# Gate and up projections of a hybrid decoder layer: three of eight row pairs as seven block products, with a reordered group and the gate function on ScalarE

## The chip, the cores and the metric

The kernel runs on one core of one Trainium2 chip. The metric is the device time of one execution in microseconds (us). A core has TensorE (PE in the rows), which multiplies; VectorE (DVE) and ScalarE (ACT), which work element by element; GpSimd (POOL); and SyncE (SP), which here issues the weight loads. The engines run their own instruction lists in order and wait for each other through semaphores.

## What is computed

One decoder layer on 256 tokens with a model width of 2048, then a final RMSNorm. Before the part that the change touches there is a combined input projection, three kinds of token mixing and an output projection. The part that matters here is the feed-forward block, whose hidden width is 5632:

```
hf = rms_norm(x, norm_ffn)
gate, up = jnp.split(hf @ w_gu, 2, axis=-1)      # w_gu: 2048 x 11264
return x + (jax.nn.silu(gate) * up) @ w_down     # w_down: 5632 x 2048
```

`silu(g)` is `g * sigmoid(g)`, which is also `0.5 * g * (1 + tanh(g / 2))`.

## The kernel before

All products are fp32-like. Each operand is split into a high part (fp32r, a rounded fp32) and a low part (the rest), and a product of blocks is three matmuls: high by high, high by low of the weights, low by high (`ff_product`, L1691). The 128 x 128 block of activations is the stationary operand, a 128 x 512 block of weights the moving one.

The gate and up projections are 11 groups of 512 columns each of gate and of up. In a group, the 2048 rows of the weights are 8 row pairs (k = 0 to 7) of 2 x 128 rows. A **unit** is one row pair of gate or of up: 128 x 1024 numbers, 512 KB, loaded by one DMA into one of four `raw` buffers. ScalarE copies it to `w_hi` (`ff_high`, L644), VectorE writes raw minus high to `w_lo` (`ff_low`, L1176), TensorE multiplies it with the two token blocks b = 0, 1 and the two row blocks: 12 matmuls. `w_hi` and `w_lo` are rings of four slots, so ScalarE may fill a slot only when TensorE has used the slot four before it (`unit_used`), and a load may refill a `raw` buffer only when VectorE has read it (`lo_ready`).

For a row pair in **seven** form (kind "seven"), gate and up of the row pair are treated together as a 2 x 2 by 2 x 2 block product and done with 7 block products instead of 8 (Winograd's form of Strassen's scheme): 21 matmuls in place of 24. It takes four slots of the ring: the gate unit, half of the up unit, and two slots with sums of weight blocks. The sums are made by three VectorE operations (`ff_weight_sums`, L1188), and are then split in high and low as well (`ff_sum_high`, L650; `ff_sum_low`, L1182). The matching sums of the activations are made once (`ff_summands`, L1127). Seven products use the four `mx` PSUM banks and three `acc` banks; after the last "seven" of a group the common parts are added to the right sums (`fold_gate`, `fold_up`, L1211 and L1222).

Group 0 has no "seven". The groups j = 1 to 10 follow the table `FF_ORDER` (L61), each entry (kind, k, i, v): row pair k, load number i, ring slot v. Here two row pairs are "seven". All engines follow the same table, each with its own work between the entries:

- After the first unit of a group, TensorE transposes the 8 blocks of the product silu(gate) * up of the group before (`act_transposed`, L1669) into `mx`; ScalarE copies them to `actT_hi` (`act_high`, L625); VectorE makes `actT_lo` (`act_low`) and four sums for the down projection (`act_sums`, L1110).
- VectorE makes the product itself (`activate_folded`, L1077): an add and a multiply for each token block, the second pair only when TensorE has finished the group.
- The gate function: ScalarE computes tanh of half the gate (`gate_tanh`, L616), VectorE finishes it with (tanh + 1) * gate (`gated`, L1067).

The activations are kept at full precision in `hT_hi` and `hT_lo`. The groups are a hardware loop with one group per turn on ScalarE, VectorE and TensorE; SyncE's list is unrolled.

Of the kernel before, what the change touches and what calls it, by code (L numbers as in the profile page):

```python
# [14 lines left out]
F32 = mybir.dt.float32  # L15
# [49 lines left out]
FF_SLOT_OF = [-4, -3, -2, -1] + [v + d for kind, _k, _i, v in FF_ORDER for d in ((0, 1) if kind == "seven" else (0,))]  # L65
# [65 lines left out]
def hybrid_layer(nc, x, norm_mix, w_in, gla_a2, gla_ab, gla_norm, ml_conv, ml_ib, ml_fb, ml_norm,  # L131
                 sgu_ln_g, sgu_ln_b, sgu_w, sgu_b, w_out, norm_ffn, w_gu, w_down, norm_final, out):
    ctx = ExitStack()
    with ctx:
# [16 lines left out]
        half_rs_h, half_rs2_h = stat[:, 18:20], stat[:, 20:22]  # L151
# [121 lines left out]
        def _(sp):  # L273
# [75 lines left out]
        def _(pool):  # L349
# [81 lines left out]
            pool.wait_ge(sem("gate_used"), 2 * NG_FF)  # L431
            pool.wait_ge(sem("x1_stored"), 16 * NB)
# [10 lines left out]
        def _(act):  # L443
# [172 lines left out]
            def gate_tanh(used, gates_read=None):  # L616
# [8 lines left out]
            def act_high(groups, c):  # L625
                act.wait_ge(sem("actT_psum"), groups)
                act.activation(actT_hi[:, bass.ds(c, 4), :].rearrange("p c t -> p (c t)"),
                               mx[:, 0:2, :].rearrange("p k n -> p (k n)"), ACT.Copy).then_inc(sem("act_hi"), 1)

            def first_gate_up():  # L630
                for k in range(2 * UPG):
# [17 lines left out]

            def ff_sum_high(j, d, v, made):  # L650

                act.wait_ge(sem("ff_w_sums"), j * 4 + (made - 4))
                act.wait_ge(unit_used, j * FF_SLOTS + (FF_BASE + v - R + 1))
                act.activation(w_hi[:, v % R, :], ff_sum[:, d, :, :].rearrange("p k n -> p (k n)"), ACT.Copy)\  # L654
                   .then_inc(hi_ready, 1)

            def gate_up(j):
                for kind, k, i, v in FF_ORDER:
                    if kind == "up" and k == 4:
                        act.wait_ge(unit_used, j * FF_SLOTS + (FF_BASE + 12))  # L660
                        act.wait_ge(lo_ready, j * FF_SLOTS + (FF_BASE + 13))
# [6 lines left out]
                    if kind == "gate" and k == 5:  # L668
                        act_high(j, j * 4 - 4)
                    if kind == "up" and k == 6:  # L670
                        act.wait_ge(sem("gate_folded"), j * 2)
                        gate_tanh(j * FF_SLOTS + (FF_BASE + 14), j * 2)

            first_gate_up()
            with act.Fori(1, NG_FF) as j:
                gate_up(j)
# [67 lines left out]
        def _(dve):  # L744
# [332 lines left out]
            def activate_folded(groups, used):  # L1077

                for b in range(NB):
# [10 lines left out]
                    dve.scalar_tensor_tensor(out=act_tok[:, b, :], in0=up_part(b), scalar=half_rs2_h[:, b:b + 1],  # L1090
# [3 lines left out]
            def activate(used, gates_done):  # L1094
# [3 lines left out]
                for b in range(NB):  # L1098
                    dve.scalar_tensor_tensor(out=act_tok[:, b, :], in0=acc[:, 2 + b, :], scalar=half_rs2_h[:, b:b + 1],
# [3 lines left out]
            def act_low(groups, c, summed=False):  # L1103
# [4 lines left out]
                   .then_inc(sem("act_lo_made" if summed else "act_lo"), 1)  # L1108

            def act_sums(j, g):  # L1110

                a11, a12_, a21_, a22_ = (mx[:, 0, c * P:(c + 1) * P] for c in (0, 2, 1, 3))
                s1, s3 = (s_32[:, g, i, :].rearrange("p g n -> p (g n)") for i in range(2))
                c = bass.ds(j * 4 - 4, 1)
                s2, s4 = (t[:, c, P:2 * P].rearrange("p c t -> p (c t)") for t in (actT_hi32, actT_lo32))
                dve.wait_ge(sem("act_lo_made"), j)
                dve.tensor_copy(s4, a21_).then_inc(sem("a21_kept"), 1)
                dve.wait_ge(sem("a21_kept"), j)
                dve.tensor_tensor(s1, a22_, s4, ALU.add).then_inc(sem("s1_made"), 1)
# [25 lines left out]

            def ff_summands_low():
# [4 lines left out]
                                  ff_sum[:, 1, :, :].rearrange("p k n -> p (k n)"), flat, ALU.subtract)\  # L1151
                   .then_inc(sem("ff_lo_ready"), 1)

            def first_gate_up():
                for k in range(2 * UPG):
# [8 lines left out]
                    if k == 11:  # L1164
                        dve.wait_ge(sem("rs_h_ready"), 1)
                        step(dve.tensor_tensor(half_rs2_h, rs_h, rs_h, ALU.mult))
                        dve.tensor_scalar(half_rs_h, rs_h, 0.5, None, ALU.mult).then_inc(sem("rs_h2_ready"), 1)
                        settle()
                        step(dve.tensor_scalar(half_rs2_h, half_rs2_h, 0.5, None, ALU.mult))
                        settle()  # L1170
                        gated(0)
                    if k == 13:
                        ff_summands()
                ff_summands_low()

            def ff_low(j, i, v, c0=0):  # L1176

                dve.wait_ge(hi_ready, j * FF_SLOTS + (FF_BASE + v + 1))
                dve.tensor_tensor(w_lo[:, v % R, c0:UC * GW], raw[:, i % R, c0:UC * GW],  # L1179
                                  w_hi[:, v % R, c0:UC * GW].bitcast(F32), ALU.subtract).then_inc(lo_ready, 1)  # L1180

            def ff_sum_low(j, d, v):  # L1182

                dve.wait_ge(hi_ready, j * FF_SLOTS + (FF_BASE + v + 1))
                dve.tensor_tensor(w_lo[:, v % R, :], ff_sum[:, d, :, :].rearrange("p k n -> p (k n)"),
                                  w_hi[:, v % R, :].bitcast(F32), ALU.subtract).then_inc(lo_ready, 1)

            def ff_weight_sums(j, i, k, opening=False):  # L1188

                a = i % R  # L1190
                for slot in range(2):
                    dve.wait_ge(loaded[a + slot], j * (16 * 2 * UPG // R) + 16 * ((U_FF + i) // R + 1))
                if k == 1:
# [664 lines left out]
```

## Time and profile before

| | us |
|---|---|
| median of 3 runs | 1102.86 (1102.61 to 1103.05) |
| the profiled execution | 1103.19 |
| its span, first to last instruction | 1101.5 |
| PE busy in the span | 1090.1 (99%) |
| DVE busy | 864.0 (78%) |
| ACT busy | 580.9 (53%) |
| mean granted TensorE clock | 0.998 of full speed |

The profile is of one execution. Matmuls overlap: a 128 x 512 one is shown as 0.39 us long, but the next one starts long before it ends, so the time of a stretch of TensorE is read from the starts. For the same reason "busy" of PE does not tell how fast it goes. DVE and ACT operations overlap a little as well (a row "x4 4.74" is four operations in 4.74 us). In the rows, "<-" after an idle time names what the engine waited for.

### The profile page before, as it was taken

The numbers are of one execution on the slowest core, as the hardware profiler recorded it, in microseconds if no ns is written. First come the engines' busy times: TensorE is split into PE (matmuls) and PEld (weight loads), VectorE is DVE, ScalarE is ACT, GpSimd is POOL, SyncE is SP. The second block draws the span as 40 slices with busy tenths as digits, with TensorE's granted clock in tenths as the row PEclk, the third lists the DMA queues.
The fourth block names the chain that finished last, engine by engine and source line by source line (L and its number), as shares of the span: only waits on it lengthen the run. The fifth ranks groups of instructions, "written<-read, shape, count | busy, mean of one in ns | idle before, by whom it ended". The sixth has DMA issues, their size and how long they took to land.

```text
span 1101.5 us, 13909 instructions
## 1 busy us (share of the span) xinstructions
PE 1090.1 (99%) x5101; PEld 906.9 (82%) x5101; DVE 864.0 (78%) x1061; ACT 580.9 (53%) x705; POOL 40.6 (4%) x68
## 2 busy tenths in 40 slices
PE   8999999999999999999999999999999999999997
PEld 7897889888888888888888888888888888888885
DVE  5556866688756557988988888889888899899896
ACT  5655545555445444545545545546455556546553
POOL 2600000000010000000000000000000000000000
PEclk9999999999999999999999999999999999999999
DMA  8765646465546575656657557566565766666663
GB/s 285 217 197 168 189 128 183 154 172 153 190 176 223 178 267 171 211 171 215 202 158 230 167 174 241 175 192 210 170 212 194 282 203 216 199 200 213 195 226 116
DMA packets 110941, 215.31 MB, mean 195 GB/s; under 512 B 6956, under 2 KB 11632, under 8 KB 110000
## 3 DMA queue, kind: packets, MB, share of 16 engines
q1 hardware_dynamic: 108976, 205.36, 59.2%
q0 software_dynamic: 1632, 8.96, 2.2%
q8 instruction: 28, 0.46, 0.2%
q10 hardware_dynamic: 288, 0.39, 0.1%
q14 instruction: 17, 0.14, 0.0%
HBM read 210.49 MB, written 4.19 MB: 195 GB/s over the span
## 4 chain that ended last, share of the span: by engine, by line
PE 96%; DVE 2%; DMA 1%; issue 1%; SPq 0%; ACT 0%; POOLq 0%; POOL 0%; ACTq 0%; DVEq 0%
PE acc L1693 11%; PE acc L1694 11%; PE acc L1695 11%; PE acc L1413 11%; PE acc L1414 11%; PE acc L1415 11%; PE acc L1758 5%; PE acc L1759 5%; PE acc L1760 5%; PE mx L1405 2%; PE mx L1693 2%; PE mx L1694 2%; PE mx L1695 2%; PE mx L1758 1%; PE mx L1759 1%; PE mx L1760 1%
## 5 line engine op out<-in xcount | busy, mean ns | idle before, releaser
L759 DVE TENSOR_TENSOR w_lo<-raw,w_hi 128x1024 fp32r<-128x1024 f32 (+2 forms) x144 | 166.7, 1169 | 117.8 <-ACT w_hi L454 117.0
L454 ACT ACTIVATE w_hi<-raw 128x1024 fp32r<-128x1024 f32 (+2 forms) x143 | 143.4, 1013 | 135.0 <-PE acc L1415 132.7
L648 ACT ACTIVATE w_hi<-raw 128x1024 fp32r<-128x1024 f32 (+1 forms) x160 | 158.4, 1005 | 94.4 <-PE acc L1695 86.7
L1693 PE MATMUL acc<-w_hi,hT_hi 128*128 128x512 f32 x520 | 203.3, 391 | 0.0
L1179 DVE TENSOR_TENSOR w_lo<-raw,w_hi 128x1024 fp32r<-128x1024 f32 (+1 forms) x160 | 180.5, 1154 | 29.0 <-ACT w_hi L648 27.2
L1694 PE MATMUL acc<-w_lo,hT_hi 128*128 128x512 f32 x520 | 202.4, 389 | 0.0
L1695 PE MATMUL acc<-w_hi,hT_lo 128*128 128x512 f32 x520 | 202.3, 389 | 0.0
L1413 PE MATMUL acc<-w_hi,hT_hi 128*128 128x512 f32 (+2 forms) x416 | 157.7, 379 | 0.0
L1415 PE MATMUL acc<-w_hi,hT_lo 128*128 128x512 f32 (+2 forms) x416 | 155.5, 374 | 0.0
L1414 PE MATMUL acc<-w_lo,hT_hi 128*128 128x512 f32 (+2 forms) x416 | 155.5, 374 | 0.0
L1695 PEld LDWEIGHTS acc<-w_hi,hT_lo 128*128 128x128 f32 x520 | 97.6, 188 | 20.5
L1693 PEld LDWEIGHTS acc<-w_hi,hT_hi 128*128 128x128 f32 x520 | 97.6, 188 | 20.0
L1694 PEld LDWEIGHTS acc<-w_lo,hT_hi 128*128 128x128 f32 x520 | 97.7, 188 | 20.0
L692 ACT ACTIVATE w_hi<-raw 128x1024 fp32r<-128x1024 f32 x88 | 83.3, 970 | 34.4 <-PE acc L1760 18.8
L1280 DVE TENSOR_TENSOR w_lo<-raw,w_hi 128x1024 fp32r<-128x1024 f32 x88 | 94.6, 1111 | 6.1 <-ACT w_hi L692 3.9
L1760 PE MATMUL acc<-w_hi,actT_lo 128*128 128x512 f32 x250 | 97.3, 389 | 0.0
L1758 PE MATMUL acc<-w_hi,actT_hi 128*128 128x512 f32 x232 | 90.5, 390 | 0.0
L1759 PE MATMUL acc<-w_lo,actT_hi 128*128 128x512 f32 x232 | 90.3, 389 | 0.0
L1415 PEld LDWEIGHTS acc<-w_hi,hT_lo 128*128 128x128 f32 x416 | 78.2, 188 | 14.0
L1413 PEld LDWEIGHTS acc<-w_hi,hT_hi 128*128 128x128 f32 x416 | 78.2, 188 | 13.9 <-ACT tok L479 0.4
L1414 PEld LDWEIGHTS acc<-w_lo,hT_hi 128*128 128x128 f32 x416 | 78.2, 188 | 13.1
L654 ACT ACTIVATE w_hi<-ff_sum 128x1024 fp32r<-128x1024 f32 x40 | 42.5, 1063 | 73.9 <-PE acc L1695 60.8
(299 smaller groups left out, 1553.3 us busy)
## 6 DMA issues: line engine op xcount, KB each, us to landing
raw<-in_w_gu SPq DMA_DIRECT2D x176, 512.0 KB, 4.2
raw<-in_w_down SPq DMA_DIRECT2D x88, 512.0 KB, 4.5
raw<-in_w_in SPq DMA_DIRECT2D x79, 512.0 KB, 3.9
raw<-in_w_out SPq DMA_DIRECT2D x32, 512.0 KB, 4.3
raw<-in_w_in SPq DMA_DIRECT2D x8, 272.0 KB, 2.8
raw<-in_w_in SPq DMA_DIRECT2D x8, 264.0 KB, 2.8
x<-in_x POOLq DMA_DIRECT2D x2, 1024.0 KB, 8.0
x_kept<-x POOLq DMA_DIRECT2D x2, 1024.0 KB, 6.1
```

Source lines behind the costliest of these rows:

```text
L648: act.activation(w_hi[:, v % R, c0:UC * GW], raw[:, i % R, c0:UC * GW], ACT.Copy).then_inc(hi_ready, 1)
L759: dve.tensor_tensor(w_lo[:, slot, 0:UC * width], raw[:, slot, 0:UC * width], w_hi[:, slot, 0:UC * width].bitcast(F32), ALU.subtract).then_ ...
L1179: dve.tensor_tensor(w_lo[:, v % R, c0:UC * GW], raw[:, i % R, c0:UC * GW], w_hi[:, v % R, c0:UC * GW].bitcast(F32), ALU.subtract).then_inc ...
L1413: pe.matmul(o, hi[:, c + i, tb], wh, start=first and i == 0, stop=False)
L1414: pe.matmul(o, hi[:, c + i, tb], wl, start=False, stop=False)
L1415: ins = pe.matmul(o, lo[:, c + i, tb], wh, start=False, stop=last and i == UC - 1)
L1693: pe.matmul(o, a[0], w[0], start=first, stop=False)
L1694: pe.matmul(o, a[0], w[1], start=False, stop=False)
L1695: return pe.matmul(o, a[1], w[0], start=False, stop=last)
L1758: pe.matmul(o, a[0], w[0], start=first, stop=False)
L1759: pe.matmul(o, a[0], w[1], start=False, stop=False)
L1760: return pe.matmul(o, a[1], w[0], start=False, stop=last)
```

## The change

Five edits in the gate and up projections:

1. A third row pair (k = 2) becomes "seven" in each of the groups 1 to 10. Its activation sums are made once, at the end of group 0 (`third_summands`), and kept in a part of `actT_hi` and `actT_lo` that is not used until the last group. The plain units of k = 2 fall away.
2. The table: three gate units stand ahead of the first "seven" instead of four, and "seven" 2 stands after the unit up 3. A group now has 22 slots instead of 20, which is not a multiple of four, so slots are numbered by the parity of the group (`ring`), and the hardware loops take two groups per turn (4 turns for groups 2 to 9; groups 1 and 10 are written out).
3. Loads are issued in order of use. The gate and up units of "seven" 0 and 1 now lie in `raw` buffers 3 and 0, so `ff_weight_sums` reads the pair as `raw[:, 3::-3, ...]`, with a negative step between two rows of 512.
4. The gate function is one ScalarE operation per token block, `Silu`; `gated` on VectorE is gone, and the scale factors are simpler.
5. VectorE's own order in a group: `activate_folded` comes after the second unit's low part instead of the third's; the weight sums of "seven" 0 come ahead of `act_low` and `act_sums`, not behind them; the copy of block a21 goes to ScalarE; `fold_gate` stands before up 6 and `fold_up` after up 7.

```
-FF_ORDER = [("gate", 2, 0, 0), ("gate", 3, 1, 1), ("gate", 4, 2, 2), ("gate", 5, 3, 3), ("seven", 0, 4, 4),
-            ("gate", 6, 6, 8), ("gate", 7, 7, 9), ("seven", 1, 8, 10)] + [("up", k, 8 + k, 12 + k) for k in range(2, UPG)]
-FF_SLOTS = 20
+FF_SUMMED = 3
+FF_ORDER = [("gate", 3, 0, 0), ("gate", 4, 1, 1), ("gate", 5, 2, 2), ("seven", 0, 3, 3), ("gate", 6, 5, 7), ("gate", 7, 6, 8),
+            ("seven", 1, 7, 9), ("up", 3, 9, 13), ("seven", 2, 10, 14)] + [("up", k, 8 + k, 14 + k) for k in range(4, UPG)]
+FF_SLOTS = 22
...
+def ring(j, v):
+    return (v + 2 * ((j[1] - 1) % 2)) % R
...
-                    act.activation(gate_s[:, b, :], acc[:, b, :], ACT.Tanh, scale=half_rs_h[:, b:b + 1])\
-                       .then_inc(sem("gate_tanh"), 1)
+                    act.activation(gate_s[:, b, :], acc[:, b, :], ACT.Silu, scale=rs_h[:, b:b + 1])\
+                       .then_inc(sem("gate_used"), 1)
...
-            def gated(tanhs):
-
-                for b in range(NB):
-                    dve.wait_ge(sem("gate_tanh"), tanhs + b + 1)
-                    dve.scalar_tensor_tensor(out=gate_s[:, b, :], in0=gate_s[:, b, :], scalar=1.0, in1=acc[:, b, :],
-                                             op0=ALU.add, op1=ALU.mult).then_inc(sem("gate_used"), 1)
...
+            def third_summands():
+
+                full = actT_lo32[:, FC - 2:FC, :]
+                a11, a21_, a12_, a22_ = (full[:, c, b * P:(b + 1) * P] for c in range(2) for b in range(NB))
+                s1, s3, s2, s4 = (third_32[:, i // 2, (i % 2) * P:(i % 2 + 1) * P] for i in range(4))
...
-                dve.tensor_tensor(ff_sum[:, 0, :, :], raw[:, a + 1, :].rearrange("p (k n) -> p k n", k=UC),
-                                  raw[:, a:a + 2, 0:GW], ALU.subtract).then_inc(sem("ff_w_sums"), 1)
+                upper = raw[:, a:a + 2, 0:GW] if b > a else raw[:, a::b - a, 0:GW]
+                dve.tensor_tensor(ff_sum[:, 0, :, :], raw[:, b, :].rearrange("p (k n) -> p k n", k=UC), upper,
+                                  ALU.subtract).then_inc(sem("ff_w_sums"), 1)
...
             def gate_up(j, opening=False, summed=True):
                 for kind, k, i, v in FF_ORDER:
                     if kind == "seven":
                         ff_weight_sums(j, i, k, opening)
+                        if k == 0 and summed:
+                            act_sums(j, bass.ds(lin(j, 1, -1), 1))
...
+                    if kind == "up" and k == 6:
+                        fold_gate(j)
...
-                    if kind == "gate" and k == 5:
-                        act_low(j, j * 4 - 4, summed)
-                        if summed:
-                            act_sums(j, bass.ds(j - 1, 1))
...
-            with pe.Fori(2, NG_FF) as j:
-                gate_up(j)
+            gate_up((None, 1), True)
+            with pe.Fori(1, NG_FF // 2) as p:
+                gate_up((p, 0))
+                gate_up((p, 1))
+            gate_up((None, NG_FF - 1))
```

How VectorE's list changes around the first "seven" of group 1 (w_lo: low part of weights; actT_lo, s: what `act_low` and `act_sums` write; ff_sum: sums of weights). Before:

```order
L1179 TENSOR_TENSOR w_lo<-raw,w_hi 128x1024 [waits w_hi_ready]
L1106 TENSOR_TENSOR actT_lo<-mx,actT_hi 128x1024 [waits act_hi]
L1117 COPY actT_lo<-mx 128x128 [waits act_lo_made]
L1119 TENSOR_TENSOR s<-mx,actT_lo 128x128 [waits a21_kept]
L1120 TENSOR_TENSOR s<-mx,actT_lo 128x128
L1122 SCALAR_TENSOR_TENSOR actT_hi<-mx,s 128x128 [waits s1_made]
L1125 TENSOR_TENSOR actT_lo<-mx,actT_hi 128x128 [waits s3_made,s2_made]
L1200 TENSOR_TENSOR ff_sum<-raw 128x1024 [waits ff_lo_ready,w_loaded1,w_loaded0]
L1203 TENSOR_TENSOR ff_sum<-raw,ff_sum 128x512 [waits ff_w_sums]
L1206 TENSOR_TENSOR ff_sum<-raw,ff_sum 128x512 [waits ff_t2]
L1179 TENSOR_TENSOR w_lo<-raw,w_hi 128x1024 [waits w_hi_ready]
```

The same place of VectorE's list after the change:

```order
L1221 TENSOR_TENSOR w_lo<-raw,w_hi 128x1024 [waits w_hi_ready]
L1243 TENSOR_TENSOR ff_sum<-raw 128x1024 [waits ff_lo_ready,w_loaded0,w_loaded3]
L1246 TENSOR_TENSOR ff_sum<-raw,ff_sum 128x512 [waits ff_w_sums]
L1249 TENSOR_TENSOR ff_sum<-raw,ff_sum 128x512 [waits ff_t2]
L1135 TENSOR_TENSOR actT_lo<-mx,actT_hi 128x768 [waits a21_kept,act_hi]
L1140 TENSOR_TENSOR actT_lo<-mx,actT_hi 128x128
L1146 TENSOR_TENSOR s<-mx,actT_lo 128x128
L1147 TENSOR_TENSOR s<-mx,actT_lo 128x128
L1149 SCALAR_TENSOR_TENSOR actT_hi<-mx,s 128x128 [waits s1_made]
L1152 TENSOR_TENSOR actT_lo<-mx,actT_hi 128x128 [waits s3_made,s2_made]
L1221 TENSOR_TENSOR w_lo<-raw,w_hi 128x1024 [waits w_hi_ready]
```

The three weight sums moved ahead of the work on the transposed blocks, the copy is gone, and the low part is made in two pieces. The buffers read are now 0 and 3.

VectorE's list from the sum slots of "seven" 1 on, in group 1, before (L1215 is the first row of `fold_gate`):

```order
L1185 TENSOR_TENSOR w_lo<-ff_sum,w_hi 128x1024 [waits w_hi_ready] x2
L1179 TENSOR_TENSOR w_lo<-raw,w_hi 128x1024 [waits w_hi_ready] x4
L1215 TENSOR_TENSOR ff_sum<-mx,ff_sum 128x512 [waits p1_kept,unit_used]
L1216 TENSOR_TENSOR acc<-acc,ff_sum 128x512
L1218 TENSOR_TENSOR ff_sum<-mx,ff_sum 128x512 [waits t6_made]
L1220 TENSOR_TENSOR acc<-acc,ff_sum 128x512 [waits t7_made]
```

And after (from the sum slots of "seven" 1 to those of "seven" 2):

```order
L1227 TENSOR_TENSOR w_lo<-ff_sum,w_hi 128x1024 [waits w_hi_ready] x2
L1221 TENSOR_TENSOR w_lo<-raw,w_hi 128x1024 [waits w_hi_ready]
L1243 TENSOR_TENSOR ff_sum<-raw 128x1024 [waits w_lo_ready,w_loaded3,w_loaded2]
L1246 TENSOR_TENSOR ff_sum<-raw,ff_sum 128x512 [waits ff_w_sums]
L1249 TENSOR_TENSOR ff_sum<-raw,ff_sum 128x512 [waits ff_t2]
L1221 TENSOR_TENSOR w_lo<-raw,w_hi 128x1024 [waits w_hi_ready]
L1221 TENSOR_TENSOR w_lo<-raw,w_hi 128x512 [waits w_hi_ready]
L1227 TENSOR_TENSOR w_lo<-ff_sum,w_hi 128x1024 [waits w_hi_ready] x2
```

Where four plain units followed "seven" 1, there is now one, and then a third "seven".

## Rows read from the trace of the kernel before

**Rows 1.** The page: busy of the engines, and the chain that ended last.
```profile
PE 1090.1 (99%) x5101; PEld 906.9 (82%) x5101; DVE 864.0 (78%) x1061; ACT 580.9 (53%) x705; POOL 40.6 (4%) x68
...
PE 96%; DVE 2%; DMA 1%; issue 1%; SPq 0%; ACT 0%; POOLq 0%; POOL 0%; ACTq 0%; DVEq 0%
```

**Rows 2.** Engine busy time in one group: stretch, length, busy us (instructions), clock, DMA.
```profile
542.40:585.70 43.30, 43.30 (x196) 35.55 (x195) 37.43 (x44) 22.51 (x25) 0.00 (x0) 1.00 0.62 194
```

**Rows 3.** Waits from 420 to 860 us: total us, times, longest.
```profile
PEld mx L1693 <- DVE w_lo L1179: 2.9, 8, 0.4
```

**Rows 4.** Timeline of PE: start, us, engine, line, operation.
```profile
499.81 0.39 PE L1693 MATMUL mx<-w_hi,ff_hi 128*128 128x512 f32 x1
...
519.99 0.39 PE L1695 MATMUL acc<-w_hi,hT_lo 128*128 128x512 f32 x1
520.21 1.08 PE L1405 MATMUL mx<-ident,act_tok 128*128 128x128 f32 x8
521.04 0.47 PE L1693 MATMUL acc<-w_hi,hT_hi 128*128 128x512 f32 x1
521.36 0.39 PE L1694 MATMUL acc<-w_lo,hT_hi 128*128 128x512 f32 x1
...
529.09 0.39 PE L1695 MATMUL acc<-w_hi,hT_lo 128*128 128x512 f32 x1
529.43 0.50 PE L1693 MATMUL mx<-w_hi,hT_hi 128*128 128x512 f32 x1
529.76 0.40 PE L1694 MATMUL mx<-w_lo,hT_hi 128*128 128x512 f32 x1
...
539.76 0.39 PE L1693 MATMUL mx<-w_hi,hT_hi 128*128 128x512 f32 x1
```

**Rows 5.** Timeline of DVE in one group.
```profile
518.60 0.68 DVE L1085 TENSOR_TENSOR up_s<-acc,up_s 128x512 f32<-128x512 f32 x1
519.32 0.75 DVE L1090 SCALAR_TENSOR_TENSOR act_tok<-up_s,stat,gate_s 128x512 f32<-128x512 f32 x1
519.98 1.22 DVE L1179 TENSOR_TENSOR w_lo<-raw,w_hi 128x1024 fp32r<-128x1024 f32 x1
...
524.03 0.29 DVE L1117 COPY actT_lo<-mx 128x128 f32 x1
...
525.56 1.23 DVE L1200 TENSOR_TENSOR ff_sum<-raw 128x1024 f32<-128x1024 f32 x1
...
528.15 1.82 DVE L1179 TENSOR_TENSOR w_lo<-raw,w_hi 128x1024 fp32r<-128x1024 f32 x2
...
537.08 1.82 DVE L1179 TENSOR_TENSOR w_lo<-raw,w_hi 128x1024 fp32r<-128x1024 f32 x2
...
542.41 4.74 DVE L1179 TENSOR_TENSOR w_lo<-raw,w_hi 128x1024 fp32r<-128x1024 f32 x4
...
568.90 1.23 DVE L1200 TENSOR_TENSOR ff_sum<-raw 128x1024 f32<-128x1024 f32 x1
```

**Rows 6.** Timeline of ACT in the same group.
```profile
521.43 1.03 ACT L627 ACTIVATE actT_hi<-mx 128x1024 f32 x1 [2.68 <-PE mx L1405]
...
539.96 1.06 ACT L654 ACTIVATE w_hi<-ff_sum 128x1024 fp32r<-128x1024 f32 x1 [1.66 <-PE acc L1695]
541.32 2.01 ACT L648 ACTIVATE w_hi<-raw 128x1024 fp32r<-128x1024 f32 x2 [0.30 <-PE acc L1695]
```

**Rows 7.** L307, the gate and up loads: one load between 530.0 and 531.3 us.
```profile
L307 SPq DMA_DIRECT2D raw<-in_w_gu x1: 368/368/368, 530.0 to 530.0; - x1
...
DMA to landing us min/median/max: 4.4/4.4/4.4
```

**Rows 8.** By line, whole trace: tanh, its completion, and a table load (ns min/median/max).
```profile
L622 ACT ACTIVATE gate_s<-acc,stat x22: 678/686/695, 412.1 to 853.7; 128x512 f32<-128x512 f32 x22
...
L1071 DVE SCALAR_TENSOR_TENSOR gate_s<-gate_s,acc x22: 679/680/689, 412.9 to 857.1; 128x512 f32<-128x512 f32 x22
...
L592 ACT ACT_TABLE_LOAD  x1: 1283/1283/1283, 227.6 to 227.6; - x1
```

More of the change, by code:

```diff
@@ L58, with lin @@
 U_DN = U_FF + NG_FF * 2 * UPG
-FF_ORDER = [("gate", 2, 0, 0), ("gate", 3, 1, 1), ("gate", 4, 2, 2), ("gate", 5, 3, 3), ("seven", 0, 4, 4),
-            ("gate", 6, 6, 8), ("gate", 7, 7, 9), ("seven", 1, 8, 10)] + [("up", k, 8 + k, 12 + k) for k in range(2, UPG)]
-FF_SLOTS = 20
+FF_SUMMED = 3
+FF_ORDER = [("gate", 3, 0, 0), ("gate", 4, 1, 1), ("gate", 5, 2, 2), ("seven", 0, 3, 3), ("gate", 6, 5, 7), ("gate", 7, 6, 8),
+            ("seven", 1, 7, 9), ("up", 3, 9, 13), ("seven", 2, 10, 14)] + [("up", k, 8 + k, 14 + k) for k in range(4, UPG)]
+FF_SLOTS = 22
 FF_BASE = U_FF + 2 * UPG - FF_SLOTS
-FF_SLOT_OF = [-4, -3, -2, -1] + [v + d for kind, _k, _i, v in FF_ORDER for d in ((0, 1) if kind == "seven" else (0,))]
+SEVEN_END = {k: v + 4 for kind, k, _i, v in FF_ORDER if kind == "seven"}
+FF_SLOT_OF = {i - R: i - R for i in range(R)}
+for _kind, _k, _i, _v in FF_ORDER:
+    FF_SLOT_OF[_i] = _v
+    if _kind == "seven":
+        FF_SLOT_OF[_i + 1] = _v + 1
+def lin(j, m, c=0):
+    p, o = j
+    return o * m + c if p is None else p * (2 * m) + (o * m + c)
+def ring(j, v):
+    return (v + 2 * ((j[1] - 1) % 2)) % R
 V_DN = FF_BASE + FF_SLOTS * NG_FF
@@ L310, in _ @@
             for j in range(1, NG_FF):
-                for kind, k, i, _v in FF_ORDER:
+                for kind, k, i, _v in sorted(FF_ORDER, key=lambda entry: entry[2]):
                     if kind == "seven":
@@ L614, in _, with gate_silu @@
                         out_high(n)
-            def gate_tanh(used, gates_read=None):
+            def gate_silu(used, gates_read=None):
                 act.wait_ge(unit_used, used)
@@ L668, in gate_up @@
                     if kind == "gate" and k == 5:
[L669 to L672, printed above, removed]
+                        act_high(lin(j, 1), lin(j, 4, -4), lin(j, 4, -4) if summed else None)
+                act.wait_ge(sem("gate_folded"), lin(j, 2))
+                gate_silu(lin(j, FF_SLOTS, FF_BASE + SEVEN_END[2]), lin(j, 2))
             first_gate_up()
-            with act.Fori(1, NG_FF) as j:
-                gate_up(j)
+            gate_up((None, 1))
+            with act.Fori(1, NG_FF // 2) as p:
+                gate_up((p, 0))
+                gate_up((p, 1))
+            gate_up((None, NG_FF - 1), summed=False)
             def down_square(n, b):
@@ L1165, in first_gate_up @@
                         dve.wait_ge(sem("rs_h_ready"), 1)
[L1166 to L1171, printed above, removed]
                     if k == 13:
                         ff_summands()
+                        third_summands()
@@ L1174, in first_gate_up @@
                 ff_summands_low()
             def ff_low(j, i, v, c0=0):
-                dve.wait_ge(hi_ready, j * FF_SLOTS + (FF_BASE + v + 1))
-                dve.tensor_tensor(w_lo[:, v % R, c0:UC * GW], raw[:, i % R, c0:UC * GW],
-                                  w_hi[:, v % R, c0:UC * GW].bitcast(F32), ALU.subtract).then_inc(lo_ready, 1)
+                dve.wait_ge(hi_ready, lin(j, FF_SLOTS, FF_BASE + v + 1))
+                dve.tensor_tensor(w_lo[:, ring(j, v), c0:UC * GW], raw[:, i % R, c0:UC * GW],
+                                  w_hi[:, ring(j, v), c0:UC * GW].bitcast(F32), ALU.subtract).then_inc(lo_ready, 1)
@@ L1188, in ff_weight_sums @@
             def ff_weight_sums(j, i, k, opening=False):
[L1190 to L1193, printed above, removed]
-                    dve.wait_ge(lo_ready, j * FF_SLOTS + (FF_BASE + 8))
+                a, b = i % R, (i + 1) % R
+                for n in (i, i + 1):
+                    dve.wait_ge(loaded[n % R], lin(j, 16 * 2 * UPG // R, 16 * ((U_FF + n) // R + 1)))
@@ L1240, in gate_up @@
                         else:
[L1241 to L1258 removed]
+                            activate_folded(lin(j, 1, -1), lin(j, FF_SLOTS, FF_BASE))
+                    if kind == "up" and k == 7:
+                        fold_up(j)
+            first_gate_up()
+            gate_up((None, 1), True)
+            with dve.Fori(1, NG_FF // 2) as p:
+                gate_up((p, 0))
+                gate_up((p, 1))
+            gate_up((None, NG_FF - 1), summed=False)
             def down_add(n, b, used):
@@ L1725, in ff_unit @@
                         a = [t[:, UC * k + c, b * P:(b + 1) * P] for t in (hT_hi, hT_lo)]
-                        w = [t[:, v % R, c * GW:(c + 1) * GW] for t in (w_hi, w_lo)]
-                        ins = ff_product(acc[:, 2 * up + b, :], a, w, (not up or b == 1) and k == 2 and c == 0,
+                        w = [t[:, ring(j, v), c * GW:(c + 1) * GW] for t in (w_hi, w_lo)]
+                        ins = ff_product(acc[:, 2 * up + b, :], a, w, (not up or b == 1) and k == FF_SUMMED and c == 0,
                                          up and k == UPG - 1 and c == UC - 1)
```

159 lines of the change are left out of this document (92 added, 67 removed).

## The prediction

> **What bounds the kernel now.** I read the page first. PE is busy for 99% of the span and holds 96% of the chain that ended last [rows 1]: a saving counts if it makes TensorE's list shorter, and anything else matters only where TensorE comes to wait for it. Next the timeline of PE in one group. From 499.81 to 519.99 us there are 89 steps from matmul to matmul, 20.18 us in all, 0.2267 us each and none longer [rows 4]. The group repeats every 43.34 us (the same VectorE row at 525.56 and 568.90, [rows 5]). So TensorE's price for a 128x512 matmul is 0.2267 us, not the 0.39 us of a row. The clock is at its upper level in this stretch (1.00, [rows 2]).
>
> Then the waits. Among all gate and up groups TensorE waits for VectorE in one place only: 8 times, 2.9 us together on the weight-load side, at the first product of "seven" 0 [rows 3]. In the timeline, VectorE's low part begins at 528.15 and lasts 1.22, so it is there at 529.37 [rows 5]; the matmul was due 0.2267 after 529.09, at 529.32. It starts at 529.43 and the next one at 529.76 [rows 4]. The steps are 0.34 and 0.33: together 0.23 us lost for an operand about 0.05 us late. I keep this as the rule of thumb for TensorE here: lateness plus about 0.15 to 0.2.
>
> Last the load of the others: in a group VectorE is busy for 37.43 of 43.30 us, ScalarE for 22.51 [rows 2]. VectorE has 5.9 us to spare, less than it seems, as its order is tied to TensorE.
>
> **Part 1, the third "seven".** It removes 3 matmuls in each of 10 groups: 30 x 0.2267 = 6.80 us off TensorE's list. I count it whole, since TensorE runs without gaps around it.
> The Trainium skill, "TensorE: Matmul & The Clock Gate" (Back-to-back issue gap), gives about 131 ns per 512-column matmul in a stream of weight loads and matmuls, and 216 ns for an isolated gap. By 131 ns the 30 matmuls would be worth 3.9 us. This trace does not agree with 131: it has 226.7 ns.
>
> What it adds to VectorE per group: two full low parts go (2 x 1.22, as in row 519.98); a full and a half low part (1.82, row 528.15), two low parts of sums (2.4, at the price of a full one each) and three weight sums (525.56 to 528.15, 2.59) come [rows 5]. That is +4.4. Off go two `gated` (2 x 0.68 with a little overlap, 1.3) [rows 8] and the copy (0.29) [rows 5]. Net +2.8: about 40.2 of some 42.8 us, 94%. ScalarE gets about +1.7 for weights and 0.3 for the copy, 24.5 us: it isn't near a limit. At 94% VectorE still isn't the bound by its sum, so the question is where its order makes TensorE wait. There are two such places.
>
> **Part 2, the first "seven" of a group.** I walk VectorE's new order on the clock of [rows 4, 5]. The last matmul of the previous group starts 12 x 0.2267 before 519.99, at 517.27, and ends 0.39 later, 517.66. VectorE's second add may start at 517.70. Then add to multiply 0.72 (518.60 to 519.32), multiply to next 0.66: 519.08. The third unit's low part, 1.17 (four in 4.74, less the last one's tail): 520.25. The weight sums, 2.59: 522.84. The low part of the transposed blocks, now in two pieces: no row has a 768-wide operation; between 0.68 (512 wide) and 1.22 (1024 wide), I take 0.95, and 0.2 to 0.29 for the small piece: 1.15. ScalarE's high part of them (521.43 + 1.03, [rows 6]) and the added copy (about 0.3) are done at 522.8, just in time. The four small sums took 1.53 with the copy (524.03 to 525.56), 1.24 without: 525.23. The low part that "seven" 0 waits for, 1.22: **526.45**. TensorE has one unit less before it: 521.36 + 23 x 0.2267 = **526.57**. Before the change, VectorE was 0.05 late here; now it is 0.12 early. So the wait of [rows 3] goes: 8 x 0.23 = **-1.84 us**. Bounds: 0 to -1.84 if the lead isn't enough, and worse if VectorE's pieces cost more (the rivals). A load hides behind this: the pair for "seven" 0 is asked for when the first unit's low part is done, over 5 us before its sums.
>
> **Part 3, the third "seven": a new wait.** It begins one unit (12 matmuls) after "seven" 1. A ring slot ties the two: the last sum slot of "seven" 1 can be filled only when TensorE has used the unit gate 7. From this trace: TensorE starts "seven" 1 at 539.76 [rows 4]; ScalarE gets the slot at 539.96 and goes on to the next unit until 542.4 [rows 6]; VectorE starts the low part of that next unit at 542.41 [rows 5]. So far nothing is changed. Now, behind one low part (1.17: 543.58) come the three sums (2.59: 546.17) and the low part for "seven" 2 (1.22): **547.39**. TensorE wants it after 21 + 12 matmuls: 539.76 + 33 x 0.2267 = **547.24**. VectorE is 0.15 late, and by the price above that costs 0.15 + 0.15 = 0.30 us in each of 10 groups: **+3.0 us**. More speed of VectorE elsewhere doesn't help, since the chain starts with TensorE itself. Bounds: 0 (the chain 0.3 quicker) to 0.6 a group, 6 us, if each of the six steps costs 0.05 more. The loads are not in it: "seven" 1's raw buffer is read at about 537.08 + 1.2 on this clock, and the second load of a close pair takes 4.4 us [rows 7], so it is there at about 542.8, and the sums begin at 543.6.
>
> **Part 4, what I price at nothing.** Silu in place of tanh: the same shape, 0.686 us [rows 8]; bounds 0 to a doubling, 1.4 us more on ScalarE. It now follows `fold_gate`; that needs 4 operations of 0.7 after the last "seven", and TensorE needs the gate banks four units (10.9 us) after it. So silu is ready some 6 us early. One table load is added at the first silu; one took 1.28 us [rows 8], and it lies in group 0, where weights are made three units (8 us) ahead. The order shows none in the loops.
> The Trainium skill, "ScalarE: Activation LUTs" (What ACT_TABLE_LOAD costs), adds a drain of about 1.4 us to each load; hidden in the same way, it would change nothing unless every group had one.
> `third_summands`: one add of 512, four of 128, one low part, about 2.7 us more on VectorE late in group 0, minus the 1.3 of `gated` and the small operations; two unit lengths ahead of TensorE. If that cover went it would cost at most 2.7 once. Order of loads: 16 x 512 KB a group as before.
>
> **Sum.** -6.80 - 1.84 + 3.0 = -5.6 us. On the profiled execution (1103.19, span 1101.5): 1097.6. The median of the runs is 0.33 below it, so **1097.3 us**. By the ends of parts 2 and 3 alone: -8.6 (1094.2) to -0.8 (1102.1).
>
> **Rivals.**
> A. *No new wait* at "seven" 2: the steps of part 3 overlap a little more than their starts show. For it: 0.15 us is thin. Against it: all steps are start to start. Then -8.6: **1094.2**.
> B. *VectorE's tied order eats the gain.* The loops now take two groups per turn, and many of VectorE's instructions take an address or a count from a register; the spacings of [rows 5] hold the cost of that only as far as the old loop had it, and the sums and the pieces of part 2 are new to their places. With 0.4 more in the walk of part 2 and 0.2 more in that of part 3, the waits are 0.28 + 0.2 = 0.48 and 0.50: -6.8 - 1.84 + 9 x 0.48 + 10 x 0.50 = +0.7, and half of such an excess gives about 1100.5. I take **1102**.
> C. *Slower: the negative step.* No row shows a read that goes backward. If it made the first sum of "seven" 0 and 1 twice as long (1.22 more), "seven" 1 would bear it: its first low part ends at 538.3 and is wanted at 539.76. "Seven" 0 wouldn't: 0.12 ahead becomes 1.10 late, 1.3 lost with the restart, 10 times. -6.8 - 1.84 + 3.0 + 13 = +7.4: **1110**. It decides from about 0.5 us more per read (1.7 in place of 1.22), where the gain is gone. Against it: two rows of 512 contiguous numbers each, with one jump between them, and the step forward costs the same 1.22 as a plain low part.
> D. *The change doesn't shorten TensorE's list*: the order shows 21 matmuls for 24, so I give this nothing.
>
> **Chances.** Forecast 0.66 (its own range 1095.5 to 1100.5), A 0.10, B 0.14, C 0.10. A measurement of this kernel tells about 0.2%, 2.2 us, from no change. Faster by more than that: nearly all of the forecast (0.63), A, and a third of B: 0.77. Within it: 0.03 + 0.08 + 0.02 of a mild C: 0.13. Slower: 0.02 of B and 0.08 of C: 0.10. The range is 1094.0 to 1101.3: below it half of A's tail, above it most of B and C.
>
> **What would show it.** Right: the same rows of a group repeat every 42.8 us; 183 matmuls a group; no wait at "seven" 0; a wait of TensorE for VectorE's w_lo at the first product of "seven" 2 of about 0.3 us, 10 times; the first weight sum still 1.22 us; one table load at about 411 us. Wrong: a weight sum over 1.7 us (C), waits of 0.4 us or more at "seven" 0 (B), TensorE waiting at another slot or for a load, or a VectorE group above 41 us of busy time.

## The result, and the profile after

The changed kernel takes 1097.72 us (median of 5, 1096.55 to 1097.83), the kernel before 1102.87 (median of 5). The ratio is 0.995, 95% interval 0.9935 to 0.9964: faster by 5.2 us. 1097.3 was predicted.

The page of the changed kernel, the span and the same two lines as in [rows 1]:

```profile
span 1096.0 us, 13959 instructions
...
PE 1084.9 (99%) x5071; PEld 902.9 (82%) x5071; DVE 888.4 (81%) x1092; ACT 598.8 (55%) x736; POOL 40.7 (4%) x68
...
PE 92%; DVE 4%; DMA 2%; issue 1%; ACT 1%; SPq 0%; POOLq 0%; POOL 0%; DVEq 0%; ACTq 0%
```

TensorE has 30 matmuls fewer. VectorE, 2% of the chain before, now has 4%: some of the chain runs through it. One group, from the transposes of one to those of the next (the columns are those of [rows 2]):

```profile
518.83:561.52 42.69, 42.67 (x192) 35.10 (x191) 39.86 (x48) 24.23 (x27) 0.00 (x0) 1.00 0.62 198
```

A group takes 42.69 us; it took 43.34 [rows 5]. VectorE is busy for 39.86 us of it, ScalarE for 24.23. The wait of [rows 3] is gone from the first "seven", and there is a new one, 10 times. In the list of waits from 420 to 860 us it is this line:

```profile
PEld mx L1734 <- DVE w_lo L1221: 4.5, 10, 0.5
```

TensorE's timeline answers to [rows 4], first at the transposes and where it enters "seven" 0, then where it enters "seven" 2:

```profile
518.83 1.03 PE L1446 MATMUL mx<-ident,act_tok 128*128 128x128 f32 x8
...
524.93 0.39 PE L1736 MATMUL acc<-w_hi,hT_lo 128*128 128x512 f32 x1
525.16 0.39 PE L1734 MATMUL mx<-w_hi,hT_hi 128*128 128x512 f32 x1
525.39 0.39 PE L1735 MATMUL mx<-w_lo,hT_hi 128*128 128x512 f32 x1
...
542.61 0.39 PE L1736 MATMUL acc<-w_hi,hT_lo 128*128 128x512 f32 x1
543.02 0.50 PE L1734 MATMUL mx<-w_hi,hT_hi 128*128 128x512 f32 x1
543.36 0.39 PE L1735 MATMUL mx<-w_lo,hT_hi 128*128 128x512 f32 x1
```

"Seven" 0 is entered without a gap: steps of 0.23 through 525.16. At "seven" 2 two steps are 0.41 and 0.34 long, where 0.2267 each is normal: 0.30 us lost. VectorE's timeline over the same chain, which answers to [rows 5]:

```profile
536.65 1.23 DVE L1227 TENSOR_TENSOR w_lo<-ff_sum,w_hi 128x1024 fp32r<-128x1024 f32 x1 [1.01 <-ACT w_hi L679]
538.01 1.23 DVE L1221 TENSOR_TENSOR w_lo<-raw,w_hi 128x1024 fp32r<-128x1024 f32 x1
539.16 1.22 DVE L1243 TENSOR_TENSOR ff_sum<-raw 128x1024 f32<-128x1024 f32 x1
540.41 0.69 DVE L1246 TENSOR_TENSOR ff_sum<-raw,ff_sum 128x512 f32<-128x512 f32 x1
541.13 0.69 DVE L1249 TENSOR_TENSOR ff_sum<-raw,ff_sum 128x512 f32<-128x512 f32 x1
541.74 1.82 DVE L1221 TENSOR_TENSOR w_lo<-raw,w_hi 128x1024 fp32r<-128x1024 f32 x2
```

VectorE idles for 1.01 us for a ring slot, then low part, three sums, low part, without a pause. The last is there at 541.74 + 1.22 = 542.96; TensorE was due at 542.61 + 0.23 = 542.84.

The list of waits of the kernel before had one more row of TensorE's weight-load side, at the transposes. It is not among the rows ahead of the prediction, and the list of the changed kernel has no such row:

```profile
PEld mx L1405 <- issue: 2.3, 9, 0.4
```

Over the whole of the two profiled executions: group 1's transposes start at 433.81 before and 433.40 after; those in the down projection at 869.91 and 863.45; the last matmul at 1093.04 and 1087.67. So the 10 groups give 6.05 us (436.10 against 430.05), 0.41 was there before group 1, and the down projection gives back 1.09 (223.13 against 224.22). The 0.41 isn't the change's: ScalarE's table load at 101.8 us before is already at 101.4 after, far ahead of any changed instruction.

### The profile page after: what moved, and what is told of

Same layout as the page of the kernel before. It is cut to its first block, busy times and chain, and to the rows that moved or that the text cites. A ratio compares the mean times of both kernels' runs of the same rounds, so it can differ in the third digit from the quotient of the medians.

```text
span 1096.0 us, 13959 instructions
## 1 busy us (share of the span) xinstructions
PE 1084.9 (99%) x5071; PEld 902.9 (82%) x5071; DVE 888.4 (81%) x1092; ACT 598.8 (55%) x736; POOL 40.7 (4%) x68
## 4 chain that ended last, share of the span: by engine, by line
PE 92%; DVE 4%; DMA 2%; issue 1%; ACT 1%; SPq 0%; POOLq 0%; POOL 0%; DVEq 0%; ACTq 0%
PE acc L1454 11%; PE acc L1455 11%; PE acc L1456 11%; PE acc L1735 10%; PE acc L1734 10%; PE acc L1736 10%; PE acc L1805 4%; PE acc L1807 4%; PE acc L1806 4%; PE mx L1734 3%; PE mx L1735 2%; PE mx L1736 2%; PE mx L1446 2%; PE mx L1805 1%; PE mx L1807 1%; PE mx L1806 1%
## 5 line engine op out<-in xcount | busy, mean ns | idle before, releaser
L1734 PE MATMUL acc<-w_hi,hT_hi 128*128 128x512 f32 x460 | 179.9, 391 | 0.0
L1735 PE MATMUL acc<-w_lo,hT_hi 128*128 128x512 f32 x460 | 179.1, 389 | 0.0
L1736 PE MATMUL acc<-w_hi,hT_lo 128*128 128x512 f32 x460 | 179.0, 389 | 0.0
L1221 DVE TENSOR_TENSOR w_lo<-raw,w_hi 128x1024 fp32r<-128x1024 f32 (+1 forms) x160 | 173.3, 1119 | 2.8
L673 ACT ACTIVATE w_hi<-raw 128x1024 fp32r<-128x1024 f32 (+1 forms) x160 | 151.5, 978 | 36.7 <-PE acc L1736 21.8
L679 ACT ACTIVATE w_hi<-ff_sum 128x1024 fp32r<-128x1024 f32 x60 | 63.8, 1063 | 78.3 <-PE acc L1736 65.2
L1736 PEld LDWEIGHTS acc<-w_hi,hT_lo 128*128 128x128 f32 x460 | 86.3, 188 | 18.0
L1734 PEld LDWEIGHTS acc<-w_hi,hT_hi 128*128 128x128 f32 x460 | 86.4, 188 | 17.7
L1735 PEld LDWEIGHTS acc<-w_lo,hT_hi 128*128 128x128 f32 x460 | 86.4, 188 | 17.6
L1456 PEld LDWEIGHTS acc<-w_hi,hT_lo 128*128 128x128 f32 x416 | 78.2, 188 | 14.1
L1454 PEld LDWEIGHTS acc<-w_hi,hT_hi 128*128 128x128 f32 x416 | 78.2, 188 | 13.8 <-ACT tok L498 0.4
L1455 PEld LDWEIGHTS acc<-w_lo,hT_hi 128*128 128x128 f32 x416 | 78.2, 188 | 13.1
```

The costliest lines, as they stand in the source:

```text
L673: act.activation(w_hi[:, ring(j, v), c0:UC * GW], raw[:, i % R, c0:UC * GW], ACT.Copy).then_inc(hi_ready, 1)
L1221: dve.tensor_tensor(w_lo[:, ring(j, v), c0:UC * GW], raw[:, i % R, c0:UC * GW], w_hi[:, ring(j, v), c0:UC * GW].bitcast(F32), ALU.subtract ...
L1454: pe.matmul(o, hi[:, c + i, tb], wh, start=first and i == 0, stop=False)
L1455: pe.matmul(o, hi[:, c + i, tb], wl, start=False, stop=False)
L1456: ins = pe.matmul(o, lo[:, c + i, tb], wh, start=False, stop=last and i == UC - 1)
L1734: pe.matmul(o, a[0], w[0], start=first, stop=False)
```

## The experiments

Each kernel was timed against the kernel before on the same chip. Medians of before were 1103.09 and 1103.14 in the two sets. Group periods are from the profiles, from transposes to transposes, one group of each (group 3).

### The order of VectorE's list alone (e2_sums_first)

```
                     if kind == "seven":
                         ff_weight_sums(j, i, k, opening)
+                        if k == 0:
+                            act_low(j, j * 4 - 4, summed)
+                            if summed:
+                                act_sums(j, bass.ds(j - 1, 1))
                     ff_low(j, i, v)
...
-                    if kind == "gate" and k == 5:
-                        act_low(j, j * 4 - 4, summed)
-                        if summed:
-                            act_sums(j, bass.ds(j - 1, 1))
```

> The kernel before, with one part of edit 5 alone: in VectorE's list the three weight sums of seven 0 stand ahead of act_low and act_sums. Nothing is left out of the computation. Theory (term of part 2: VectorE was late at seven 0 because its list held the work on the transposed blocks, which waits for ScalarE, ahead of the sums): TensorE's wait at the first product of seven 0 goes, 0.23 us in each of 8 groups, 1101.0 us, group period 43.1 instead of 43.34. Rival (the wait went because there was one unit less to fill, or because of the gate function, not because of this order): 1102.9, period 43.34.

Measured: 1101.52 us (11 runs), ratio 0.9984 (0.9975 to 0.9993). The line of [rows 3] is gone and the group takes 43.14 us. Four moved lines alone take that wait away and are worth 1.6 us. VectorE used to idle for ScalarE's high part of the transposed blocks with the sums behind it, for 1.45 us in this row of the kernel before; now it makes the sums in that time:

```profile
522.65 1.23 DVE L1106 TENSOR_TENSOR actT_lo<-mx,actT_hi 128x1024 f32 x1 [1.45 <-ACT actT_hi L627]
```

### The gate function alone (e1_silu)

```
-                    act.activation(gate_s[:, b, :], acc[:, b, :], ACT.Tanh, scale=half_rs_h[:, b:b + 1])\
-                       .then_inc(sem("gate_tanh"), 1)
+                    act.activation(gate_s[:, b, :], acc[:, b, :], ACT.Silu, scale=rs_h[:, b:b + 1])\
+                       .then_inc(sem("gate_used"), 1)
...
-                        if k == 7:
-                            gated(j * 2)
```

> The kernel before, with the gate function alone changed: Silu on ScalarE, no gated on VectorE. Nothing is left out. Theory (part 4: hidden on both engines; gated stood far from any place where TensorE waits): no change, 1102.9 us, group period 43.34, the wait at seven 0 still 0.23 us in 8 groups, one table load in group 0. Rival (1.3 us less on VectorE brings it forward at seven 0, so this edit and not the order took the wait away): 1101.0.

Measured: 1102.90 us (11 runs), ratio 0.9997 (0.9988 to 1.0006). The wait at "seven" 0 stands as before, from the waits of this run:

```profile
PEld mx L1685 <- DVE w_lo L1173: 2.9, 8, 0.4
```

1.3 us less work for VectorE in each group, and nothing of it reaches TensorE: the work stood between places where VectorE waits anyway.

### A shorter list for TensorE alone (e6_fewer_matmuls)

```
+                        if up and k == 5 and b == 0 and c == 0:
+                            continue
                         ins = ff_product(acc[:, 2 * up + b, :], a, w, ...
```

> The kernel before, where one block product (3 matmuls) of the unit up 5 is left out in each of groups 1 to 10, so the output isn't the reference's. No other engine's work changes. Theory: a matmul taken off TensorE's list is worth its step of 0.2267 us, 30 are worth 6.8: 1096.1 us. Rival (VectorE's tie to TensorE, or the wait at seven 0, which grows when TensorE gets there sooner relative to VectorE, keeps part): 1097.5 or more. A matmul at 131 ns, as the Trainium skill's page TensorE: Matmul & The Clock Gate (Back-to-back issue gap) has it, would give 1098.9.

Measured: 1096.47 us (5 runs, 1095.10 to 1097.82), ratio 0.9936 (0.9923 to 0.995): 6.6 us. The group takes 42.68 us, 0.66 less. The rival's loss wasn't there, nor was the price of 131 ns that the expectation cites: a matmul off this list is worth its step of 0.2267. In the profile the 10 groups give 6.9 (436.10 against 429.23) and the down projection gives 1.6 back (224.69).

### All but the third "seven" (e5_two_sevens)

```
-FF_SUMMED = 3
+FF_SUMMED = 2
...
-FF_SLOTS = 22
+FF_SLOTS = 20
...
-    return (v + 2 * ((j[1] - 1) % 2)) % R
+    return v % R
```

(with `FF_ORDER` of the kernel before, and without `third_summands`)

One part of edit 5 goes back with the table: `activate_folded` is tied to the unit gate 4, which is the third unit again. The pairs of "seven" 0 and 1 lie in `raw` buffers 0 and 1 again, so nothing is read backward.

> The changed kernel without the third seven: two row pairs as seven, the table of slots of the kernel before, all the rest as in the changed kernel (Silu, VectorE's own order, loads in order of use, two groups per turn of the loops). Nothing is left out. Theory (the sum: the other edits give only the 1.84 of the old wait; the third seven gives 6.8 less 3.0): 1101.0 us, no wait at seven 0, group period 43.1. Rival (the other edits hold more of the gain, or the longer loops cost time): below 1100, or 1102.9 and more.

Measured: 1100.79 us (11 runs), ratio 0.9977 (0.9968 to 0.9987). The groups take 43.05 and 43.14 us in turn, and there is no wait at "seven" 0. So the third "seven" with its table is worth 1100.79 - 1097.72 = 3.1 us, measured in two sets of runs; 6.8 - 3.0 = 3.8 was reckoned. In the profiles the 10 groups do give 3.9 (433.98 against 430.05), and the changed kernel gives 1.0 back in the down projection (223.22 against 224.22). All the other edits together give about 2.3, and two groups per turn of the loops cost nothing that shows (43.10 on average, 43.14 in e2).

### The new wait, made larger (e4_adjacent)

```
-            ("seven", 1, 7, 9), ("up", 3, 9, 13), ("seven", 2, 10, 14)] +
+            ("seven", 1, 7, 9), ("seven", 2, 9, 13), ("up", 3, 11, 17)] +
```

> The changed kernel, with seven 2 directly behind seven 1, up 3 after it. Nothing is left out. Theory: the same chain now stands against 21 matmuls, 4.76 us. VectorE saves one low part, so it is about 1.5 us late instead of 0.15, and with the restart of 0.15 TensorE loses 1.65 us in each of 10 groups instead of 0.30: 1111.2 us, group period 44.0. Rival (the loss of 0.30 is a fixed price of entering that seven, such as the change of PSUM bank, not lateness of VectorE): 1097.7, no difference.

Measured: 1112.95 us (5 runs), ratio 1.009 (1.0076 to 1.0103). The group takes 44.26 us. TensorE and VectorE where "seven" 2 is entered:

```profile
542.89 0.39 PE L1736 MATMUL acc<-w_hi,hT_lo 128*128 128x512 f32 x1
544.88 0.50 PE L1734 MATMUL mx<-w_hi,hT_hi 128*128 128x512 f32 x1 [1.60 <-DVE w_lo L1221]
545.22 0.40 PE L1735 MATMUL mx<-w_lo,hT_hi 128*128 128x512 f32 x1
```

```profile
539.65 1.23 DVE L1227 TENSOR_TENSOR w_lo<-ff_sum,w_hi 128x1024 fp32r<-128x1024 f32 x1 [1.01 <-ACT w_hi L679]
541.01 1.23 DVE L1243 TENSOR_TENSOR ff_sum<-raw 128x1024 f32<-128x1024 f32 x1
...
543.61 1.82 DVE L1221 TENSOR_TENSOR w_lo<-raw,w_hi 128x1024 fp32r<-128x1024 f32 x2
```

Due at 543.12, ready at 544.83: 1.71 late, and 1.88 lost (1.99 + 0.34 less two steps of 0.2267). 1.5 and 1.65 were expected; the first sum waits for the end of VectorE's own low part (540.88), 0.1 to 0.2 later than the spacing I had used. The loss follows the lateness; it isn't a fixed price of entering a "seven".

### The third "seven" one unit later (e3_seven_later), and why that failed (e8_later_less_dve)

```
-            ("seven", 1, 7, 9), ("up", 3, 9, 13), ("seven", 2, 10, 14)] + ... range(4, UPG)]
+            ("seven", 1, 7, 9), ("up", 3, 9, 13), ("up", 4, 10, 14), ("seven", 2, 11, 15)] + ... range(5, UPG)]
...
-                    if kind == "up" and k == 6:
+                    if kind == "up" and k == 7:
                         fold_gate(j)
```

> The changed kernel, with seven 2 one unit later in the table: up 3, up 4, seven 2, up 5 to 7; fold_gate moves from ahead of up 6 to ahead of up 7 so that TensorE need not wait for up 6. Nothing is left out. Theory (the new wait comes from the chain: slot of gate 7 free, ScalarE, VectorE low, low, sums, low, against 33 matmuls): with 45 matmuls in front VectorE is over 1 us early, the wait of 0.30 us in 10 groups goes, 1094.7 us, group period 42.4 instead of 42.69. Rival 1 (VectorE as a whole is at its limit, 94% busy): the wait only moves to another slot, 1097.7. Rival 2 (the later end of seven 2 makes fold_gate and silu late, TensorE waits for the gate banks or for up 7): slower than the changed kernel.

Measured: 1102.58 us (11 runs), ratio 0.9992 (0.9983 to 1.0001): a miss. The wait at "seven" 2 did go, but the group takes 43.24 us, from 519.49 to 562.73, and the next one 43.10, in turn. Two other places of TensorE have become late, the transposes and "seven" 0:

```profile
519.14 0.39 PE L1736 MATMUL acc<-w_hi,hT_lo 128*128 128x512 f32 x1
519.49 1.09 PE L1446 MATMUL mx<-ident,act_tok 128*128 128x128 f32 x8
...
525.66 0.39 PE L1736 MATMUL acc<-w_hi,hT_lo 128*128 128x512 f32 x1
526.35 0.50 PE L1734 MATMUL mx<-w_hi,hT_hi 128*128 128x512 f32 x1 [0.30 <-DVE w_lo L1221]
526.69 0.39 PE L1735 MATMUL mx<-w_lo,hT_hi 128*128 128x512 f32 x1
```

VectorE in the same stretch:

```profile
509.39 0.69 DVE L1258 TENSOR_TENSOR ff_sum<-mx,ff_sum 128x512 f32<-128x512 f32 x1 [0.65 <-ACT ff_sum L687]
...
516.57 0.69 DVE L1105 TENSOR_TENSOR up_s<-acc,up_s 128x512 f32<-128x512 f32 x1
...
525.08 1.82 DVE L1221 TENSOR_TENSOR w_lo<-raw,w_hi 128x1024 fp32r<-128x1024 f32 x2
```

From `fold_gate` (509.39), which must wait for the end of "seven" 2, to the low part for "seven" 0 (525.08 + 1.22), VectorE has 16.9 us of work and no idle time. TensorE wants that low part at 525.66 + 0.23 = 525.89, 16.5 us after `fold_gate` began: 0.41 late. In the changed kernel the same stretch has one unit more. VectorE begins it at 506.40 and ends it at 524.78, 18.4 us with 0.30 of idle time in it, and TensorE wants the result 18.8 us after the beginning: 0.38 early. So the move took 2.3 us from the time at hand and only 1.5 from VectorE's stretch, 1.17 of it the low part of one unit. Rival 1 was right in kind, for a stretch and not for the group. Run e8 tests that reading by taking 1.1 us of VectorE's work out of the stretch:

```
-                dve.tensor_tensor(acc[:, 0, :], acc[:, 0, :], p1, ALU.add)
+                dve.tensor_tensor(acc[:, 0, 0:32], acc[:, 0, 0:32], p1[:, 0:32], ALU.add)
...
-                dve.tensor_tensor(acc[:, 1, :], acc[:, 1, :], t7, ALU.add)
+                dve.tensor_tensor(acc[:, 1, 0:32], acc[:, 1, 0:32], t7[:, 0:32], ALU.add)
```

> The kernel of run e3_seven_later, where the two adds of fold_gate into acc work on 32 columns instead of 512, so the output isn't the reference's: VectorE has about 1.1 us less to do in each group, behind seven 2, and nothing else changes. Theory (e3 lost its gain because VectorE's list from fold_gate to the low part of the next seven 0 runs without a gap and begins one unit later; it was 0.41 late at seven 0 and 0.12 late at the transposes): both waits go, group period 42.4 instead of 43.24, 1094.8 us. Rival (the time went into the gate banks or into ScalarE's silu, or into loads): 1101 to 1102.6, no change.

Measured: 1094.24 us (4 runs), ratio 0.992 (0.9904 to 0.9935). The group takes 42.39 us and TensorE waits nowhere in it. VectorE's stretch behind the last "seven" was the cause. The shorter adds of e8 also let the silu begin sooner, so the run alone doesn't exclude rival 2. The rows of e3 do: from 509.39 on VectorE has no idle time, so it waits neither for the silu nor for a load.

### The chain shortened: faster than both (e7_split_low)

```
+                if split:
+                    dve.tensor_tensor(w_lo[:, ring(j, v), 0:GW], raw[:, i % R, 0:GW],
+                                      w_hi[:, ring(j, v), 0:GW].bitcast(F32), ALU.subtract).then_inc(sem("third_half"), 1)
+                    c0 = GW
...
+                if k == 2:
+                    pe.wait_ge(sem("third_half"), lin(j, 1))
+                    ff_product(mx[:, 2, :], a11, w(0, 0), first, last)
+                    pe.wait_ge(lo_ready, lin(j, FF_SLOTS, FF_BASE + v + 1))
```

> The changed kernel, with one step of part 3's chain cut: VectorE makes the low part of the gate unit of seven 2 in two pieces of 512 columns, and TensorE's first product of seven 2 waits for the first piece only. Nothing is left out. Theory (TensorE loses 0.30 us there because VectorE's low part is 0.12 late): the piece is ready about 0.5 us sooner, so TensorE is no longer late there; the extra piece costs VectorE 0.07 and the later slots of seven 2 have leads of only 0.1 to 0.4, so perhaps 0.05 to 0.1 is lost again: 1095.2 us (1094.7 to 1096.2), group period 42.4 to 42.5 instead of 42.69. Rival (VectorE at 94% busy is the bound, not this chain): the wait turns up at another slot, 1097.7.

Measured: 1095.18 us (5 runs, 1094.77 to 1095.49), ratio 0.9924 (0.991 to 0.9938). TensorE enters "seven" 2 on time. In its waits a shorter one is left, a slot further on, at the first product that uses the weight sums:

```profile
PEld mx L1738 <- DVE w_lo L1231: 2.1, 10, 0.3
```

```profile
544.53 0.44 PE L1738 MATMUL mx<-w_hi,actT_hi 128*128 128x512 f32 x1
544.81 0.40 PE L1739 MATMUL mx<-w_lo,actT_hi 128*128 128x512 f32 x1
```

```profile
543.20 2.35 DVE L1231 TENSOR_TENSOR w_lo<-ff_sum,w_hi 128x1024 fp32r<-128x1024 f32 x2
```

There one step is 0.28 in place of 0.23, although the operand is complete at 543.20 + 1.22 = 544.42 and the matmul, due at 544.53, starts on time. The group takes 42.43 us, 0.26 less than in the changed kernel. This is the fastest of the kernels that compute everything, about 2.5 us below the changed one.

## Why the prediction was right, step by step

- **30 matmuls, -6.80.** Right: -6.6 alone, 0.66 a group (e6).
- **The old wait, -1.84.** Right: no gap at "seven" 0. The two steps of 0.34 and 0.33 lose 0.22 rather than 0.23, and the eight waits 1.7 in all. VectorE was reckoned to be ready 0.12 before it was wanted; in the trace it is earlier still, 523.56 + 1.22 = 524.78 against 525.16:

```profile
523.56 1.82 DVE L1221 TENSOR_TENSOR w_lo<-raw,w_hi 128x1024 fp32r<-128x1024 f32 x2
```

  Alone it is worth 1.6 (e2). The part of the walk that was too dear was the small sums, which overlap more once the copy is gone: from the 768-wide piece to this row 2.0 us, where 2.39 were reckoned. That the whole 1.84 came is in part luck: in e7 an operand 0.11 early still costs 0.05 us, so a lead of 0.12, as reckoned, would by these rows have kept some 0.04 a group. Which edit does it was left open in the prediction; the order of the sums does it alone, the gate function does nothing (e1).
- **The new wait, +3.0.** Right to the tenth: 0.12 late for 0.15 reckoned, 0.30 lost, 10 times. Lengthening the chain's deficit (e4) and shortening the chain (e7) moved the time as the chain says.
- **Sum over the groups.** -6.80 - 1.84 + 3.0 = -5.6; measured -6.05. Most of the rest is at the transposes: from group 2 on the step from the transposes to the next matmul is 0.79 in place of 0.83 to 0.85, and in group 10 a step of 0.33 ahead of them is back at 0.23. That is the second row in the list of waits of before, to which the prediction gave no term. VectorE's product of the group before is complete 0.92 ahead of the transposes after the change (517.91 against 518.83), and was 0.14 ahead before it (519.32 + 0.75 = 520.07 against 520.21); that this lead makes the difference is argued, not tested.
- **The number.** 1097.3 against 1097.72 is closer than the terms are: the groups gave 0.4 us more than the sum, and the down projection took 1.09 back in the profiled execution. By this reckoning (an estimate) an execution without that gap takes 1096.6, 0.7 below the forecast; the two errors have opposite signs, and that they cancel is luck.
- **Priced at nothing.** The silu has 0.686 us like the tanh, and the one table load that it adds lies at 411.2 us:

```profile
L641 ACT ACTIVATE gate_s<-acc,stat x22: 680/686/691, 412.5 to 851.0; 128x512 f32<-128x512 f32 x22
L641 ACT ACT_TABLE_LOAD  x1: 1283/1283/1283, 411.2 to 411.2; - x1
```

  The step backward costs nothing, so rival C falls. All 30 first sums, wrapped (20) or not (10), take the same:

```profile
L1243 DVE TENSOR_TENSOR ff_sum<-raw x30: 1218/1219/1220, 433.3 to 838.1; 128x1024 f32<-128x1024 f32 x30
```

- **Not foreseen.** In the profiled execution the down projection takes 1.09 us longer. There is one gap in TensorE's list that isn't in the trace of before:

```profile
879.75 0.39 PE L1807 MATMUL acc<-w_hi,actT_lo 128*128 128x512 f32 x1
880.95 0.50 PE L1805 MATMUL mx<-w_hi,actT_hi 128*128 128x512 f32 x1 [0.81 <-DVE w_lo L1321]
```

  VectorE's sum before it waited for a load:

```profile
877.01 1.23 DVE L1339 TENSOR_TENSOR gate_s<-raw 128x1024 f32<-128x1024 f32 x1 [1.65 <-DMA raw<-in_w_down]
```

  Two loads issued at 869.5 and 870.1 took up to 6.8 us to land; the corresponding pair before took up to 5.5. Early in the down projection such a step of 0.9 to 1.7 us stands in the profiles of the changed kernel, e3, e4, e6 and e7, and not in those of the kernel before, e1, e2, e5 and e8. Four of the five kernels beside the changed one whose TensorE list is 30 matmuls shorter have it, and none of those with the full list. e6 changes none of VectorE's work, so the new order of VectorE isn't needed for it; e8 has the shorter list and no gap, so that list alone doesn't always bring it. The five runs of the changed kernel lie at 1096.55 and 1096.75, and at 1097.72 to 1097.83, about as far apart as this gap. That it is this gap that parts them, and whether the shorter list makes it more frequent, stays open: a run without profile has no rows, and no run tests it. It isn't simply the earlier start of the stage: e8 has no gap and starts it at 860.42, e3 has one and starts at 868.43.

The rival B gave half of the right idea: VectorE's tied order can eat the whole gain, but it did so in e3, where I had moved the third "seven" without redoing the walk from its end to the next "seven" 0.

## What to carry to other kernels

With in-order engines around a ring of slots, ask neither how busy an engine is nor how much work an edit takes off it, but walk from each event that ties it to the bound engine (slot free, bank complete) to the operand that engine wants next, and compare with the matmuls in between. 1.3 us less work a group gave nothing, four moved lines gave 1.6 us, and a half-size first piece of an operand gave 2.5. When a block of work is moved in a cyclic schedule, redo the walk of the stretch behind it as well as the one ahead of it.

## What the runs showed of the hardware

A late operand costs TensorE its lateness and about 0.17 us more, over the whole range seen: 0.05 late lost 0.22 [rows 4], 0.12 lost 0.30, 0.41 lost 0.57 (e3: 0.69 + 0.34 less two steps), 1.71 lost 1.88 (e4). The surplus lies in the first matmul's own start (0.05 after the operand is complete) and in the step behind it (0.34 in place of 0.23).

It doesn't begin at zero lateness: 0.11 early still lost 0.05 (e7, a first matmul on time and a step of 0.28). All five fit one line: the loss is the time by which the operand misses a point about 0.16 us ahead of the matmul's due start. An operand 0.38 us early ("seven" 0 after the change) costs nothing. When a walk ends with a lead under 0.2 us, price the rest of that 0.16.
